# First stage of a two-block transformer kernel: tokens loaded ahead of the conditioning blocks, and the work on them ahead of the first conditioning sum

## The reference

```python
c_act = jax.nn.silu(c)
mod = (c_act @ ada_w[l] + ada_b[l])[:, None, :]
sh_t, sc_t, g_t, sh_c, sc_c, g_c = jnp.split(mod, 6, axis=-1)
h = rms_norm(x, tm_pre_g[l]) * (1.0 + sc_t) + sh_t
y = token_mixer(h, w_in[l], ...)
```

## Time and profile before

| | us |
|---|---|
| median of 3 runs | 1668.8 |
| lowest and highest run | 1668.79 and 1670.48 |
| the profiled execution | 1672.08 |
| its span | 1670.1 |
| PE busy | 1616.4 (97%) |
| DVE busy | 922.8 (55%) |
| ACT busy | 614.2 (37%) |
| mean granted clock of PE in the profiled execution | 0.986 |

### The profile page before, as it was taken

How to read it: one execution, slowest core, us unless ns; L and a number is a source line. 1 busy time by engine, 2 the same in 40 slices (tenths; PEclk the granted TensorE clock), 3 DMA queues, 4 the chain that set the end, 5 groups by cost and what they waited for, 6 DMA issues and landing times.

```text
span 1670.1 us, 20144 instructions
## 1 busy us (share of the span) xinstructions
PE 1616.4 (97%) x7710; PEld 1313.0 (79%) x7710; DVE 922.8 (55%) x1275; ACT 614.2 (37%) x788; POOL 239.4 (14%) x132
## 2 busy tenths in 40 slices
PE   5999999989999799999999999999999999999998
PEld 5887678767888488888888887877788888888887
DVE  5559355437786744444432667766335656556333
ACT  4333353233234443333322532344543433333223
POOL 1210023220002011011000000343342111110000
PEclk9999999989999899999999999999999999999999
DMA  9233113205773123333222234222123333333221
GB/s 336 76 101 101 51 51 101 76 26 188 240 227 101 51 76 100 100 100 91 98 90 99 76 101 136 64 76 77 51 76 101 112 85 92 100 100 100 101 92 59
DMA packets 192228, 170.44 MB, mean 102 GB/s; under 512 B 9543, under 2 KB 180900, under 8 KB 192164
## 3 DMA queue, kind: packets, MB, share of 16 engines
q1 hardware_dynamic: 174240, 150.16, 29.0%
q10 hardware_dynamic: 16948, 16.89, 3.2%
q0 software_dynamic: 976, 2.52, 0.4%
HBM read 165.54 MB, written 2.10 MB: 100 GB/s over the span
## 4 chain that ended last, share of the span: by engine, by line
PE 90%; DVE 6%; ACT 2%; DMA 1%; issue 1%; SPq 0%; POOL 0%; DVEq 0%; ACTq 0%
PE bank L1283 22%; PE bank L1285 21%; PE bank L1284 21%; PE bank L1290 6%; PE bank L1292 6%; PE bank L1291 6%; DVE w_lo L1890 1%; DVE work L2028 1%; PE bank L1375 1%; PE bank L1833 1%; DMA work<-in_x 1%; PE bank L1597 1%; ACT w_hi L724 1%; PE bank L1387 1%; PE bank L1818 1%
## 5 line engine op out<-in xcount | busy, mean ns | idle before, releaser
L1283 PE MATMUL bank<-h_hi,w_hi 128*128 128x512 f32 (+1 forms) x1568 | 616.6, 393 | 8.2 <-DVE h_lo L1908 4.0
L1285 PE MATMUL bank<-h_hi,w_lo 128*128 128x512 f32 (+1 forms) x1568 | 607.1, 387 | 0.0
L1284 PE MATMUL bank<-h_lo,w_hi 128*128 128x512 f32 (+1 forms) x1568 | 606.2, 387 | 0.0
L1890 DVE TENSOR_TENSOR w_lo<-w_raw,w_hi 128x2048 fp32r<-128x2048 f32 x102 | 234.6, 2300 | 265.0 <-ACT w_hi L724 264.7
L1283 PEld LDWEIGHTS bank<-h_hi,w_hi 128*128 128x128 f32 x1568 | 296.4, 189 | 87.7 <-issue 22.9
L724 ACT ACTIVATE w_hi<-w_raw 128x2048 fp32r<-128x2048 f32 x131 | 250.1, 1909 | 280.2 <-PE bank L1292 171.1
L1285 PEld LDWEIGHTS bank<-h_hi,w_lo 128*128 128x128 f32 x1568 | 296.1, 189 | 60.6
L1284 PEld LDWEIGHTS bank<-h_lo,w_hi 128*128 128x128 f32 x1568 | 296.6, 189 | 58.1 <-issue 1.0
L638 POOL TENSOR_TENSOR w_lo<-w_raw,w_hi 128x2048 fp32r<-128x2048 f32 x29 | 134.3, 4632 | 546.8 <-ACT w_hi L724 546.8
L1290 PE MATMUL bank<-w_hi,y_hi 128*128 128x512 f32 x352 | 137.9, 392 | 0.9 <-DVE work L2378 0.9
L1292 PE MATMUL bank<-w_lo,y_hi 128*128 128x512 f32 x352 | 137.0, 389 | 0.0
(11 more groups left out here) (286 smaller groups left out, 1604.6 us busy)
## 6 DMA issues: line engine op xcount, KB each, us to landing
w_raw<-in_w_in SPq DMA_DIRECT2D x94, 512.0 KB, 4.4
w_raw<-in_ffn_w_up SPq DMA_DIRECT2D x44, 512.0 KB, 4.5
w_raw<-in_w_up SPq DMA_DIRECT2D x44, 512.0 KB, 4.7
work<-in_ada_w ACTq DMA_DIRECT2D x16, 1024.0 KB, 7.9
w_raw<-in_ffn_w_down SPq DMA_DIRECT2D x22, 512.0 KB, 4.0
w_raw<-in_w_down SPq DMA_DIRECT2D x22, 512.0 KB, 4.0
work<-in_ada_w SPq DMA_DIRECT2D x8, 1024.0 KB, 11.7
w_raw<-in_w_o SPq DMA_DIRECT2D x8, 512.0 KB, 4.5
```

The costliest lines, as they stand in the source:

```text
L1283: pe.matmul(dst, w_hi[s][:, at:at + n], hi, start=first, stop=False, skip_group_check=onto)
L1284: pe.matmul(dst, w_hi[s][:, at:at + n], lo, start=False, stop=False, skip_group_check=onto)
L1285: return pe.matmul(dst, w_lo[s][:, at:at + n], hi, start=False, stop=last, skip_group_check=onto)
L1890: dve.tensor_tensor(w_lo[u % 2][:, :], raw[u % 2][:, :], w_hi[u % 2][:, :].bitcast(FP32), ALU.subtract)\
```

## The change

On SP's queue the four token blocks are issued ahead of conditioning blocks 0 and 4. On PE, `ada_begun(0)` and `ada_ended(0)` move behind both groups of transposes and the matmul on the diagonal. On DVE the diagonal is made ahead of `ada_sum(0)`. On ACT four tiles are copied ahead of `rstd` and of the split of the first weights (three before), the split comes behind `rstd`, and the last four tiles are copied at one go before `norm_hi`. No instruction is added or taken away.

```diff
+            for tt in range(TT):
+                sp.dma_start(x_tok[:, tt, :], A["x"][0, tt * P:(tt + 1) * P, :]).then_inc(sem(f"x_in{tt}"), 16)
             for n in (0, 4):
                 ada_load(sp, n)
-            for tt in range(TT):
-                sp.dma_start(x_tok[:, tt, :], A["x"][0, tt * P:(tt + 1) * P, :]).then_inc(sem(f"x_in{tt}"), 16)
...
-            x_copied(range(3))
-            split(0)
+            x_copied(range(4))
             t = T["ss0"][0]
             wait_full(act, t)
             release(act.activation(rstd[:, :], bank[t.bank][:, :], ACT.Copy, scale=float(D)), t)
-            x_copied(range(3, 5))
-            norm_hi(0, range(2))
-            x_copied(range(5, KT))
-            norm_hi(0, range(2, 6))
+            split(0)
+            x_copied(range(4, KT))
+            norm_hi(0, range(6))
...
-            ada_begun(0)
             for tt in range(TT):
                 pe.wait_ge(sem(f"x_in{tt}"), 16)
             x_turned(range(4))
-            pe.wait_ge(sem("eps_set"), 2)
-            ada_ended(0)
             t = T["ss0"][0]
             wait_free(pe, t)
             pe.wait_ge(sem("x_diagonal"), 1)
             done(pe.matmul(bank[t.bank][:, :], const("ones_d"), tbuf[:, 0, :], start=True, stop=True), t)
             x_turned(range(4, KT))
+            ada_begun(0)
+            pe.wait_ge(sem("eps_set"), 2)
+            ada_ended(0)
             weights_ready(u)
...
-            ada_sum(0, ada_pairs[0])
             dve.wait_ge(sem("x_rms"), 1)
             dve.tensor_tensor(tbuf[:, 0, :].rearrange("p (a b) -> p a b", a=TT), ident.unsqueeze(1).broadcast_to([P, TT, P]),
                               rstd_tok.unsqueeze(2).broadcast_to([P, TT, P]), ALU.mult).then_inc(sem("x_diagonal"), 1)
+            ada_sum(0, ada_pairs[0])
             lo(U["sc"])
             ada_pair(0)
```

## The result

| | changed kernel | kernel before |
|---|---|---|
| median, us | 1673.68 (12 runs) | 1670.35 (12 runs) |
| lowest to highest | 1669.35 to 1676.17 | 1668.79 to 1672.18 |
| profiled execution, its span | 1673.42, 1671.4 | 1672.08, 1670.1 |

The ratio is 1.0019 with an interval of 1.0010 to 1.0028. Forecast were 1669.3 within 1666.8 to 1672.6. The median is 1.1 us above the range. "Within 0.2%" held, barely. When both kernels ran again (experiment 1) the ratio was 1.0008. The forecast said 0.5.

What follows compares the result with a forecast made beforehand. PE was taken to carry the span, the first stage ending on near-equal DVE and PE chains. PE's longer run (+0.6) and ACT's copies (-0.1) on the median 1668.8 gave 1669.3 us, range 1666.8 to 1672.6.

Steps and rivals of the forecast that it cites:

- What bounds the kernel: PE carries the span, busy 1616.4 of 1670.1 us; first stage ends on DVE's and PE's chains, block 7 fixed at 40.88.
- Part 1: SP's queue: tokens land by 10.6 us, blocks 0 and 4 by 18.9; all behind them keeps its place.
- Part 2: Root mean square on ACT: squares end at 16.2 to 16.6 us, diagonal there at 17.7, 3.7 us earlier.
- Part 3: PE's order: work queued behind the diagonal runs from 17.7; first pair done at 26.7 to 28.2 us, middle 27.4.
- Part 4: DVE meanwhile: weights' low part ready at 26.1, PE later; norm pair 0 begins at 27.8 us, 0.6 later.
- rival A: No PE limit, weights bind: norm pair 0 at 26.5, 0.7 us earlier; total 1668.5 to 1668.8; chance 0.18.
- Part 5: From norm pair 0 to the end: a delay passes through whole; SP's vanished 3.9 us wait costed at nothing.
- the sum: Whole kernel: +0.6 for PE's longer run, -0.1 for ACT's copies, so +0.5 on the median 1668.8: 1669.3 us.
- B: PE's clock rises one group later, 1.2 GHz up to third block's matmuls: 3.1 us later, 1671.9; chance 0.09.
- C: Slower by over 0.2%: clock returns only after the first weight unit; 8.4 us with B's delay, 1677; chance 0.07.
- D: Tokens not early, landing only at 14: diagonal about 18.9, norm pair 0 1.2 us later than forecast, 1670.5; chance 0.05.
- E: Over 0.2% faster: half-clock stretch here would have to vanish (worth 0.23) and another further back as well; chance 0.05.

Runs made afterwards that it cites:

- Experiment 7: Kernel before with one added 512-column matmul, read by nobody, behind first_unit(3) on PE: 1672.75 us, ratio 1.0010.
- experiment 5: POOL's 868 KB of constants issued behind DVE's second sum, in either kernel: changed kernel 1672.96 us, ratio 1.0009; kernel before 1671.45, ratio 1.0000.
- experiment 2: Changed kernel with 16 further transposes behind ada_ended(0), filling PE's idle time ahead of block 5: 1673.26 us, ratio 1.0012.
- experiment 3: Unread 512-column matmuls added on PE: three groups in the changed kernel, 1673.60 us, ratio 1.0016; two in the kernel before, 1671.47, ratio 1.0007.

## Why the prediction was wrong

**What bounds the kernel** held. Experiment 7 shows that the end of the stage passes through, and experiment 5 that block 7 is a fixed point.

**Part 1** was right on the tokens (10.6 forecast, 10.81 PE's start) and wrong in one clause: that all behind them keeps its place. Blocks 0 and 4 were there at 19.2 to 19.8 in the five traces, not at 18.9; the weights came 0.3 us later on average and block 6 0.8. This is the first step that failed. The same bytes in another order went at a lower rate from 12 to 24 us (352 to 356 GB/s against 367 to 371), and one 8 KB transfer of instructions, which used to fall behind block 6, fell ahead of it. That these two are the cause rests on the traces; no run takes either away. It took sum 2 from about 34.6 (34.56 to 34.68 in five of the six traces of the kernel before and its variants with the constants in their place; 35.21 in the sixth) to 34.92 to 35.22 in the five with the new one, each of these with a DMA wait of 0.30 to 0.92 us. I had costed the reordering of a full queue as neutral because its sum was the same; the trace of before had the rates (342, 367, 348 GB/s) from which to ask why they differ. Norm pair 0, by contrast, was 0.4 us earlier on average (26.73 to 27.34 in the five; 27.23 to 27.89 in the six).

**Part 2** was right: diagonal done at 17.7 forecast, 17.92.

**Part 3** had the mechanism and missed a size. PE ran without idling from 17.98 to 25.6, not to 27.4: the 16 conditioning matmuls took 1.84 us and not 3.54. The clock had risen earlier than the 24.7 to 27.3 taken over from before. In this trace only the durations tell it (3.21 us for the transposes begun at 19.84, 1.84 behind them), since the clock column reads 1.00 from 12 to 24 us in both kernels, also where rows are as slow as at half clock. In the traces of experiments 1 and 2 the column does show it, 0.50 from about 16.5 to 23.7 and 23.0; there the transposes took 3.62 us and the 16 matmuls 2.22 and 2.03. The conditioning matmuls were the mis-sized term.

**Part 4** therefore took the wrong one of two limits: the weights' low part, not PE, set norm pair 0. They landed at 22.56 instead of 21.88, the split no longer stood behind copies (it began at 22.59, before at 22.70), and norm pair 0 began at 27.12. Forecast were 27.8. The copies had held the split up by 0.8 us, not by the 0.1 to 0.2 that Part 4 gave them; the later landing took 0.7 of it. The weights as the limit are rival A's outcome, 0.6 us later than A gave it because of Part 1. A's reason did not hold: PE was not at the higher clock at 17.98, since the two matmuls on the diagonal took 1.86 us from start to start, as at the lower clock before (1.85).

**Part 5**, that a delay passes whole, held. But norm pair 0 had none to pass. What passed was block 6's. SP's wait for the transposes is gone in the changed kernel, as forecast, and brought nothing: block 7's matmuls began at 41.42, against 40.97. That block 7 lands no earlier without the wait was right (41.1; 40.8 before). PE's chain then set the last pair (50.95, 0.47 us of waiting; 50.06 and 0.23 before). In four traces (the changed kernel twice, its filling, and its variant without the instruction) the stage is +0.90, +0.07, +0.88 and +0.56, on average 0.6. Against 0.1 for the four of the kernel before that makes half a microsecond. With either group spread by 0.8 to 1.0 this is an estimate, not clear of nothing; if it holds, the +0.5 of the sum came out for the wrong reason, by luck.

**The basis** was the second error in size: 1668.8, a median of three runs, is 1.5 us below what twelve gave. It is a third of the distance between forecast and median (4.4 us). The profiled execution lay 3.3 over it, which should have been read as doubt about the basis, and the range should have gone up by it. The range also did not keep its own rule: above B's 1671.9 it adds 0.7 us, not the 1 to 1.7 that it names.

**What no step had** is the instruction. "No instruction is added or taken away" is true of the code and false of the program: moving an operation past another also moved the waits it carries. That costs 1.0 us (plus or minus 0.6), and the place found for it lies some 500 us behind the change. With the stage's 0.5 this makes 1.5 of the 2.2 measured. The remaining 0.7 is within the error of the measurement, and what it is stays open. No place was found for it: the half-clock stretches also move by themselves between executions of one kernel, as between 170 and 243 us, where a repeat of before took 3.1 us more.

**The rivals.** A's limit came, with another time and for another reason. B, the clock up later, did not come: it was up earlier. But it fell again at 26, which no rival had. I expected PE's steady work to hold it, and in experiment 2 this kind of work didn't. That it cost little is what experiment 3 suggests. C (a clock at half beyond 50) and D (tokens late) did not come. E looked for its gain in a half-clock stretch further back; such a stretch did matter, with the other sign.

## What to carry to other kernels

Reordering the loads of a full queue is not neutral: look at the packet sizes and the rate by stretch, and at which load a transfer of another queue, instructions included, holds up. The load that an engine waits for must not be that one. Before costing a reordering of operations at nothing, compare the instruction count of each version, for the waits move with the operations, and one instruction on an engine that is not the bottleneck can shift wake-ups far behind. And when a forecast lies within 0.2%, its basis needs more runs than three, and no single trace of either kernel decides between explanations that differ by less than two traces of the same kernel do.

## What was unexpected of the hardware

One empty instruction early in DVE's stream lengthened a wake-up of DVE at 555 us by 0.35 us (5.78 to 6.13) in every trace, and its removal shortened it again. The page lists two DMA queues of kind "instruction" in each kernel, one with 43 packets and 0.70 MB, one with 21 and 0.17 MB. The Trainium skill, "Runtime: NRT & Kernel Launch", "Instruction fetch mechanics", says that an engine's instructions are fetched in blocks of 256 (16 KB), mostly hidden. The first queue's packets are of that size here; the second's are of 8 KB. A wait that meets the edge of a block would fit a shift by one instruction, but no run shows that the late wake-up is a fetch: the 8 KB transfer near 557 us comes 1.1 to 1.4 us behind the end of ACT's instruction with the extra instruction and without it, after DVE has begun.

That such transfers are not always hidden is what the landings of the first stage suggest: the block beside the 8 KB transfer landed 3.5 to 3.8 us behind the one before it and not 3.0, in sixteen of eighteen traces.

PE's clock fell to 0.50 while PE was busy for 3.00 of 3 us with transposes and matmuls of one column (experiment 2). By the durations it had risen during transposes (19.84 to 22.89, first trace of the changed kernel), with two matmuls of 512 columns just ahead of them; in experiment 2 itself it rose at 23.0, right behind them. With real matmuls strewn in it was 1.00 from 31.7 to 45 us (experiment 3).

From 12 to 16 us, the constants and the tokens' packets together moved at 393 GB/s, the constants and the conditioning blocks' smaller packets at 357.
